# A 32-byte move of the split weights' high halves in a two-model fp32 kernel

## The reference, cut to what matters

```python
def reference(x, ..., final_norm_w_2):
    x = first_block(x, norm_mix, w_in, ...)     # proj = h @ w_in[i] ... (silu(gt) * up) @ w_ffn_out[i]
    return second_block(x, norm_mix_w_2, ...)   # u = h @ w_in ... swiglu(h, w_gate_up, w_down)
```

## The kernel before, in words

| tile | address | by 256 | by 64 |
|---|---|---|---|
| w_raw | 16512 | 128 | 0 |
| w_hi | 32944 | 176 | 48 |
| w_lo | 49392 | 240 | 48 |
| h_hi | 74000 | 16 | 16 |
| h_lo | 82224 | 48 | 48 |
| g_hi | 170032 | 48 | 48 |
| g_lo | 178352 | 176 | 48 |
| f_hi | 117744 | 240 | 48 |
| f_lo | 140336 | 48 | 48 |
| r, s, m, o, yv, cv, ys, high and low | (several) | 224 | 32 |

## Time and profile before

### The profile page before, as it was taken

One profiled execution on the slowest core, in us unless ns is written; L12 is line 12 of the kernel. 1 busy time (PEld: TensorE's weight loads), 2 busy tenths in 40 slices (PEclk: granted clock), 3 DMA queues, 4 the chain that ended last, 5 costly groups with the idle time before them and its releaser, 6 DMA issues.

```text
span 2155.2 us, 47946 instructions
## 1 busy us (share of the span) xinstructions
PE 2131.1 (99%) x18740; PEld 2073.5 (96%) x18740; DVE 1639.8 (76%) x2627; ACT 1215.0 (56%) x1825; POOL 54.7 (3%) x53
## 2 busy tenths in 40 slices
PE   9999999999999999999999999999999999999998
PEld 8999999999999999899999999999899999999998
DVE  8997877987678766788947877766678947877774
ACT  6656544556656445446658845445446658845444
POOL 0000000000000000000002200000000002200000
PEclk9999999999999999999999999999999999999999
DMA  6444655644456556554544456556554544465553
GB/s 249 157 135 151 205 186 185 201 153 147 138 167 219 188 188 210 170 169 142 176 157 154 150 193 208 186 188 211 173 166 147 174 159 147 149 195 186 186 191 130
DMA packets 102976, 376.54 MB, mean 175 GB/s; under 512 B 11680, under 2 KB 11808, under 8 KB 102304
## 3 DMA queue, kind: packets, MB, share of 16 engines
q1 hardware_dynamic: 101664, 368.66, 51.9%
q10 hardware_dynamic: 1152, 5.58, 0.7%
HBM read 373.14 MB, written 1.05 MB: 174 GB/s over the span
## 4 chain that ended last, share of the span: by engine, by line
PE 90%; DVE 6%; ACT 2%; issue 1%; DMA 0%; DVEq 0%; ACTq 0%
PE acc L764 25%; PE acc L766 24%; PE acc L765 24%; DVE w_lo L1799 2%; PE acc L883 1%; PE acc L885 1%; PE acc L884 1%; PE acc L828 1%; PE acc L830 1%; PE acc L829 1%; ACT w_hi L1317 1%; PE mid L1120 1%; PE mid L1219 1%; DVE pr L2558 0%; PE mid L951 0%
## 5 line engine op out<-in xcount | busy, mean ns | idle before, releaser
L1799 DVE TENSOR_TENSOR w_lo<-w_raw,w_hi 128x1024 fp32r<-128x1024 f32 x694 | 847.7, 1226 | 321.8 <-ACT w_hi L1317 313.6
L1317 ACT CAST w_hi<-w_raw 128x1024 fp32r<-128x1024 f32 x694 | 723.8, 1046 | 542.2 <-PE acc L766 480.8
L764 PE MATMUL acc<-h_hi,w_hi 128*128 128x256 f32 x2096 | 599.7, 286 | 0.1
L765 PE MATMUL acc<-h_lo,w_hi 128*128 128x256 f32 x2096 | 588.9, 281 | 0.0
L766 PE MATMUL acc<-h_hi,w_lo 128*128 128x256 f32 x2096 | 585.7, 279 | 0.0
L764 PE MATMUL acc<-g_hi,w_hi 128*128 128x256 f32 x1456 | 412.3, 283 | 0.8 <-DVE w_lo L1799 0.7
L765 PE MATMUL acc<-g_lo,w_hi 128*128 128x256 f32 x1456 | 407.7, 280 | 0.0
L766 PE MATMUL acc<-g_hi,w_lo 128*128 128x256 f32 x1456 | 407.4, 280 | 0.0
L764 PEld LDWEIGHTS acc<-h_hi,w_hi 128*128 128x128 f32 x2096 | 393.7, 188 | 6.3 <-issue 5.0
L765 PEld LDWEIGHTS acc<-h_lo,w_hi 128*128 128x128 f32 x2096 | 395.3, 189 | 0.5
L766 PEld LDWEIGHTS acc<-h_hi,w_lo 128*128 128x128 f32 x2096 | 395.6, 189 | 0.0
(11 more groups left out here) (444 smaller groups left out, 3450.0 us busy)
## 6 DMA issues: line engine op xcount, KB each, us to landing
w_raw<-weights_d SPq DMA_DIRECT2D x695, 512.0 KB, 3.6
p<-p_d ACTq DMA_DIRECT2D x3, 1080.0 KB, 8.3
rdec<-decay_d ACTq DMA_DIRECT2D x2, 768.0 KB, 5.0
p<-p_d SPq DMA_DIRECT2D x1, 1024.0 KB, 10.7
out_d<-work SPq DMA_DIRECT2D x4, 256.0 KB, 2.4
x_all<-x_d SPq DMA_DIRECT2D x1, 516.0 KB, 4.5
w_raw<-weights_d SPq DMA_DIRECT2D x2, 256.0 KB, 5.8
x_all<-x_d SPq DMA_DIRECT2D x1, 512.0 KB, 6.2
```

Source lines behind the costliest of these rows:

```text
L764: mm(dst, wh, hi[:, k, :], start=first and j == 0, stop=False)
L765: mm(dst, wh, lo[:, k, :], start=False, stop=False)
L1317: nc.scalar.copy(w_hi[:, slot, :], w_raw[:, slot, :]).then_inc(hi_done, 1)
L1799: tt(w_lo[:, slot, :], w_raw[:, slot, :], w_hi[:, slot, :].bitcast(F32), SUB).then_inc(lo_v, 1)
```

## The change

The call that places `rtok` moves from behind that of `w_hi` to the front of it. `rtok` goes from byte 49344 to 32928. `w_hi` begins at 32976 in place of 32944: remainder 208 by 256 in place of 176, 16 by 64 in place of 48. `w_lo` and all tiles behind it stay where they are. No instruction, loop, wait or transfer is added, removed or moved; three kinds of instruction get another address for `w_hi` (the rounding copy that writes it, the subtraction that reads it, the weight loads and the matmuls of `slab_rows` that read it), and two kinds another one for `rtok`.

```diff
         w_raw = place("w_raw", [P, RING, SLAB])
         gain2 = place("gain2", [P, KD])
+        rtok = place("rtok", [P, 2])
         w_hi = place("w_hi", [P, RING, SLAB], F32R, lead=4)
-        rtok = place("rtok", [P, 2])
         w_lo = place("w_lo", [P, RING, SLAB], F32R, lead=4)
```

## The result

The changed kernel takes 2163.16 us (median of 20 runs, 2159.89 to 2165.71), the kernel before 2158.57 us in the 20 runs taken in turn with them (2155.76 to 2161.37). The ratio is 1.0021, interval 1.0015 to 1.0026: slower by 4.6 us, about where a change can first be told from none. The predicted time, 2160.5 us, is 2.7 us too low and the range holds the result. Part of that closeness comes from where the forecast started: it was added to a median of three runs, 2160.33 us, which lies 1.8 us above that of the 20 runs. As a change the forecast was +0.2 us against +4.6, and "no change within 0.2%" (4.3 us) is missed by a hair.

What follows compares the result with a forecast made beforehand. TensorE was taken as the bound, products times their start distance, with some 3% waits for the split. Terms -2.3 (h), +2.3 (g and f), +0.2 (s, r, m and others) gave +0.2 us: 2160.5 us, range 2152 to 2175.

Steps and rivals of the forecast that it cites:

- no change within 0.2%: Likeliest case for the whole kernel: time within 4.3 us of before, by mirror, nothing or longer split operations; chance 0.60.
- Parts (1) to (3): New addresses for `rtok`, the copy writing w_hi and the subtraction reading w_hi: each claimed to cost zero.
- (2): Copy writing w_hi: another rounding copy gave the same fixed 196 ns, so a moved target costs zero.
- longer split operations: Case that copy and subtraction get longer: together +3 us, 2163.5 us, counted within the 0.60 for no change.
- Part (4): TensorE's weight loads and streamed weights at w_hi's new address: -2.3 + 2.3 + 0.2 = +0.2 us.
- differs from 117.8 by more than 0.3 ns: Sign that the weight-load part is wrong: start distances in g, f or s stretches off by this, without idle time before products.
- h's excess: Products with h start 118.14 ns apart against 117.78 for g; these 0.36 ns were assumed to come from address distance.
- mirror image: Address patterns by 64 swap: h falls to 117.78 ns, -2.3 us; g and f rise to 118.14, +2.3 us.
- stands on both legs: Claim that the forecast holds either way: 2160.5 us if h's extra 0.36 ns come from distance, 2160.3 if not.
- The slower rival: TensorE's weight load and activation stream conflict: +11 us, 2171, deciding from 4.3 us; chance 0.23.
- The tail beyond the range: Every block on some 15,400 products gets the bad or good spacing: +34 or -68 us, neither end likely.
- The faster rival: Another start wins back part of 9 ns lost per product: -0.5 ns each, -8 us, 2152; chance 0.17.

Runs made afterwards that it cites:

- The `rtok` run: Kernel before with only `rtok` moved, to the end of memory, w_hi staying at 176: 2157.57 us, ratio 0.9997.
- the blocks with one distance for all: TensorE alone, 64 blocks of 72 products, all weights and activations at one distance, 0 to 252 in steps of 4: 113.34 to 123.4 ns a product.
- 256 mapped pairs: TensorE alone, w_hi at 176 and w_lo at 240, high and low activation each at every multiple of 16 by 256: 115.5 to 120.1 ns a product.
- distance 112: Kernel before with w_hi and w_lo at 160, and h, g and f at 16, 112 bytes further on by 256: 2113.24 us, ratio 0.9792.
- The runs with TensorE alone: Kernels of only TensorE work on operands written beforehand, at varied addresses; with w_hi moved from 176 to 208, f went from 117.75 to 120.00 ns.
- second profile: The changed kernel run and profiled once more, unaltered: 2162.04 us.
- h moved: Kernel before with activations moved: f to 240/64, g to 240/160, h to 16/64: 2158.48 us, ratio 1.0001.

## Why the prediction came out as it did

**Parts (1) to (3), zero each: right.** The `rtok` run moves nothing (0.9997, interval about 1), the copy is 1047 ns and the subtraction 1226, each within 1 ns. The argument for (2) couldn't have shown it, though: a line through two points leaves the same rest at both whatever the target costs, so the zero was a guess that held. The chance for longer split operations went to something that didn't happen.

**Part (4), the place and the kind: right; the price: wrong.** The effect sits in TensorE's pace, without idle time, and h gained what others lost. But by the prediction's own sign ("differs from 117.8 by more than 0.3 ns") part (4) was wrong, and the chain's shares, said to stay "as now", went from 90% to 95% TensorE. The step that carried the sum, "that h's excess comes from the distance" taken by 64 and turned into a mirror image, failed:

| | forecast, ns | measured, ns | forecast, us | measured, us |
|---|---|---|---|---|
| h | -0.36 | -0.81 | -2.3 | -5.1 |
| g | +0.36 | +0.74 in three stretches | | +2.4 |
| f | +0.36 | +2.2 | | +4.7 |
| g and f | | | +2.3 | +7.1 |
| s, m, r | 0 to +0.9 | 0 or +1.1 | +0.2 | about 0 to +1.6 |
| sum | | | +0.2 | +2.4 to +3.6 |

h does lose its excess and more, so the excess was one of distance; but the distances don't repeat by 64, as the blocks with one distance for all show (119.87, 117.77, 118.70, 117.79 at 0, 64, 128, 192), and g and f, which I put together as one pattern, aren't alike. They had the same pace before though their distances by 256 differ, and 117.8 is the commonest pace (122 of the 256 mapped pairs): agreement between a few placements was read as indifference to placement. The likeliest case, no change within 0.2%, given 0.60, did not come; the slower one, given 0.23, did, just above its bound of 4.3 us. The final error is small because gain and loss still offset one another and because the median that the forecast started from was 1.8 us high. Both are luck, and the forecast's own sentence on it ("stands on both legs") claimed more than two legs of one assumption can bear.

**The slower rival** had the right mechanism as far as the runs can see it: a price on TensorE's own two reads, nothing else at work, deciding "from 0.66 ns on g and f alone". It was (7.1 us) / 6480 = 1.1 ns on these, less h's gain, which this rival did not foresee. The tail beyond the range, "every block the bad or the good spacing", had the pattern right and was set aside too soon. In ns the spacings of the earlier trace rows are 359, 347 and 359. At 208 f's blocks all take the long spacing, 360 ns, and at distance 112 all take 340. What it had wrong was to take from the old address that the long and the short block make up for one another at a new one. **The faster rival** was wrong for 208 but right that a part of the 11 ns beyond one pass is a matter of addresses: 4.4 ns of them come back at distance 112.

**The read port and the start to start.** By the section "A bandwidth-pool intuition that's wrong" of the Trainium skill's page "SBUF — State Buffer" the weight load has a read port of its own. The prediction took from this that the place of the weights would be free. The runs with TensorE alone disagree with that reading as far as pace goes: 117.75 against 120.00 ns for f with only w_hi moved. They don't show whether the meeting point is a port, a bank or something in the engine. By "Wait — 56ns, not 53.3ns?" of the page "TensorE: Matmul & The Clock Gate" of the Trainium skill 256 columns would be an estimated 109.2 ns; the least that any placement here gave is 113.32.

**What stays open.** Of the 4.6 us between the medians the paces give 2.4 (second profile, s and m at 117.78) to 3.6 (first). The spans of the two profiles, less 1.5 us for each half-clock stretch, are 3.8 and 3.3 us above that of the first profile of before. The other 1 us or so is not explained. Part of it may be half-clock stretches that are more frequent by chance or by the change: 17 of the changed kernel's 20 runs have a mean clock of 0.998 or less, of the kernel before 40 of 62. Why a distance has the pace that it has, and what of the entry picks one of several, is also open; the runs show only that both matter.

## What to carry to other kernels

Read a TensorE-bound kernel by the distance of starts in steady stretches, activation by activation: group means hid this effect and busy shares diluted it. Where products reload their weights each time, byte remainders of weights and activations against one another are a tuning parameter worth 2% here. A kernel in which TensorE works alone finds candidates, but try each with several entries, take one on which all entries agree, and then read its paces in the whole kernel: distances 64 and 112 both agreed in ten entries, and only 112 held. And when two placements have the same pace, that says nothing yet about a third.

## What the runs showed of the hardware that was not expected

- A product of 256 columns with its weight load took 113.3 to 123.4 ns by addresses, with no other engine at work. Common values are 115.5, 117.8, 118.9 and 120.0 (two thirds of 256 mapped pairs). With w_hi at 176 all tiles moved together by 32, 64 or 128 bytes change nothing, and f's pairs moved by 256 or 512 bytes keep their pace within 0.1 ns.
- In the steady stretches that were read at 1 ns the distances between blocks of three products repeat in a fixed cycle: 340 ns 311 times of 311 at distance 112, 360 ns 161 times of 161 for f after, a cycle of five for h after, 347 and 359 in turn for g before.
- For some pairs how the stretch is entered decides among two or three of these paces, and the pace then holds for hundreds of products (g 118.52 over 935, s 118.88 over 286 and 117.74 over 288 in one execution).
- The granted clock fell to 1.2 GHz for some 3.4 us after a stretch of small matmuls with idle time, at the same two places of the kernel but not in each execution; 16 products at the lower clock cost 1.5 us.
- At 1.2 GHz the h products start 213 to 214 ns apart in the profiles of four placements (before, changed, h moved, distance 112), which is 256 columns at that clock. The excess that depends on addresses, 6.7 ns and more at 2.4 GHz, was not seen there.
